# Feed-forward of two stacked transformer blocks: low halves of the summed x blocks moved from GpSimd to VectorE, and one block product of the first pair of units in whole fp32

## What is computed

```python
def first_block(x, ...):
    for l in range(DEPTH):                      # DEPTH = 2
        x = x + FFN_HALF * swiglu(rmsnorm(x, ffn1_norm[l]), ffn1_w_in[l], ffn1_w_out[l])
        x = x + hybrid_mixer(rmsnorm(x, mix_norm[l]), ...)
        x = x + FFN_HALF * swiglu(rmsnorm(x, ffn2_norm[l]), ffn2_w_in[l], ffn2_w_out[l])
    return x

def swiglu(h, w_in, w_out):
    gate, up = jnp.split(h @ w_in, 2, axis=-1)  # 1024 -> 2 x 2816
    return (jax.nn.silu(gate) * up) @ w_out     # 2816 -> 1024
```

## Time and profile before

| | before |
|---|---|
| median of 3 runs | 2645.51 us (2645.24 to 2645.69) |
| profiled execution | 2645.64 us, its span 2643.5 us |
| PE busy | 2615.1 us (99%), 16043 matmuls |
| PEld busy | 2307.5 us (87%) |
| DVE busy | 2036.6 us (77%) |
| ACT busy | 1551.3 us (59%) |
| POOL busy | 212.3 us (8%) |
| HBM read | 466.09 MB |

### The profile page before, as it was taken

One profiled execution on the slowest core, in us unless ns is written; L12 is line 12 of the kernel. 1 busy time (PEld: TensorE's weight loads), 2 busy tenths in 40 slices (PEclk: granted clock), 3 DMA queues, 4 the chain that ended last, 5 costly groups with the idle time before them and its releaser, 6 DMA issues.

```text
span 2643.5 us, 38649 instructions
## 1 busy us (share of the span) xinstructions
PE 2615.1 (99%) x16043; PEld 2307.5 (87%) x16043; DVE 2036.6 (77%) x2041; ACT 1551.3 (59%) x1707; POOL 212.3 (8%) x178
## 2 busy tenths in 40 slices
PE   9999999999999999999999999999999999999998
PEld 7889999978878899999788789999788789999787
DVE  8887754698799687447998995676997995676887
ACT  6656674465555567644556555555655555655654
POOL 1000170010010003400101000000100100000100
PEclk9999999999999999999999999999999999999999
DMA  6746555466465555545656465544755646543673
GB/s 214 240 156 199 162 149 170 136 215 229 153 226 175 168 167 156 177 133 182 227 168 230 158 206 179 152 144 152 238 192 189 201 160 192 161 135 129 218 234 105
DMA packets 394925, 474.23 MB, mean 179 GB/s; under 512 B 28855, under 2 KB 360959, under 8 KB 394496
## 3 DMA queue, kind: packets, MB, share of 16 engines
q1 hardware_dynamic: 390334, 469.86, 54.9%
q10 hardware_dynamic: 4418, 1.90, 0.3%
HBM read 466.09 MB, written 5.64 MB: 178 GB/s over the span
## 4 chain that ended last, share of the span: by engine, by line
PE 86%; DVE 9%; ACT 2%; issue 1%; DVEq 1%; DMA 0%; ACTq 0%; SPq 0%
PE bank L421 26%; PE bank L423 26%; PE bank L422 26%; DVE w_lo L1207 2%; PE bank L983 1%; DVE w_lo L408 1%; DVE conv_acc L2142 1%; PE bank L563 1%; ACT w_hi L1103 1%; DVE sum_t_t L1257 1%; PE bank L1806 1%; PE bank L1782 1%; DVEq L2944 0%; DVE part L2942 0%; DVEq L2146 0%
## 5 line engine op out<-in xcount | busy, mean ns | idle before, releaser
L421 PE MATMUL bank<-w_hi,xn_hi 128*128 128x512 f32 (+2 forms) x1664 | 599.5, 360 | 0.4
L423 PE MATMUL bank<-w_hi,xn_lo 128*128 128x512 f32 (+2 forms) x1664 | 589.9, 355 | 0.0
L422 PE MATMUL bank<-w_lo,xn_hi 128*128 128x512 f32 (+2 forms) x1664 | 589.3, 354 | 0.0
L408 DVE TENSOR_TENSOR w_lo<-raw,w_hi 128x2048 fp32r<-128x2048 f32 (+2 forms) x190 | 411.9, 2169 | 199.6 <-ACT w_hi L402 199.2
L1207 DVE TENSOR_TENSOR w_lo<-raw,w_hi 128x2048 fp32r<-128x2048 f32 x192 | 448.5, 2336 | 8.7 <-ACT w_hi L1103 8.6
L1103 ACT ACTIVATE w_hi<-raw 128x2048 fp32r<-128x2048 f32 x192 | 367.2, 1912 | 135.4 <-DMA raw<-in_ffn_w_out 42.1
L402 ACT ACTIVATE w_hi<-raw 128x2048 fp32r<-128x2048 f32 (+3 forms) x199 | 359.6, 1807 | 71.9 <-PE bank L423 69.4
L421 PE MATMUL bank<-xn_hi,w_hi 128*128 128x256 f32 (+1 forms) x1376 | 396.9, 288 | 1.0 <-DVE w_lo L408 1.0
L422 PE MATMUL bank<-xn_lo,w_hi 128*128 128x256 f32 (+1 forms) x1376 | 389.0, 283 | 0.0
L423 PE MATMUL bank<-xn_hi,w_lo 128*128 128x256 f32 (+1 forms) x1376 | 389.0, 283 | 0.0
L421 PEld LDWEIGHTS bank<-w_hi,xn_hi 128*128 128x128 f32 x1664 | 315.0, 189 | 46.0 <-issue 2.9
(11 more groups left out here) (392 smaller groups left out, 4262.8 us busy)
## 6 DMA issues: line engine op xcount, KB each, us to landing
raw<-in_w_in SPq DMA_DIRECT2D x122, 1024.0 KB, 5.3
raw<-in_ffn_w_in SPq DMA_DIRECT2D x126, 512.0 KB, 5.3
raw<-in_ffn_w_out SPq DMA_DIRECT2D x44, 1024.0 KB, 5.1
raw<-in_ffn_w_down SPq DMA_DIRECT2D x44, 1024.0 KB, 5.1
raw<-in_ffn_w_gate SPq DMA_DIRECT2D x64, 512.0 KB, 4.5
raw<-in_ffn_w_up SPq DMA_DIRECT2D x64, 512.0 KB, 5.6
block<-in_ffn_w_in SPq DMA_DIRECT2D x48, 512.0 KB, 7.2
block<-in_ffn_w_gate SPq DMA_DIRECT2D x24, 512.0 KB, 6.6
```

The costliest lines, as they stand in the source:

```text
L408: dve.tensor_tensor(in_order(kind, slot, w_lo), as_loaded(kind, slot), in_order(kind, slot, w_hi).bitcast(F32), ALU.subtract).then_inc(s_l ...
L421: pe.matmul(out, a_hi, b_hi, start=start, stop=False, skip_group_check=check)
L422: pe.matmul(out, a_hi, b_lo, start=False, stop=False, skip_group_check=check)
L423: return pe.matmul(out, a_lo, b_hi, start=False, stop=stop, skip_group_check=check)
```

## The change

The low halves of the four summed x blocks are made on DVE. `mixed_lo(0)` and `mixed_lo(1)` stand in the first ones, `mixed_lo(3)` and `mixed_lo(2)` in the first pair. ACT makes the four high halves in one go, in the order 0, 1, 3, 2, ahead of the first hidden unit's high half. `t3` of the first pair is no item any more: it is neither split nor given a slot. PE multiplies the sum `mixed[2]` with the sum of weights in `b12`, both in float32, in four matmuls (`whole_product`) that count a semaphore of their own, `s_whole`, on which the reload of `b12` and the sum `u3` wait. The list of items has 41 entries. ACT takes `hi` of dn 1 between its two gates of unit 1. GpSimd's program keeps only the first mixer's work.

```diff
+WHOLE = ("t3", TWOS[0])
@@ ffn_items
-            out += [("b11", u)] + downs + [(k, u) for k in ("b21", "t1", "t2", "b22", "t3", "t4")]
+            out += [("b11", u)] + downs + [(k, u) for k in ("b21", "t1", "t2", "b22", "t3", "t4") if (k, u) != WHOLE]
@@ raw_freed
-            i = self.items.index(("t3" if u == TWOS[0] else "b22", u))
+            i = self.items.index(("t4" if u == TWOS[0] else "b22", u))
@@ ffn_sp, other_blocks
-                block(b12, 0, u + 1, p.base + (FFN_AT["t3", u - 3] + 1 + START), s_block12)
+                if ("t3", u - 3) == WHOLE:
+                    block(b12, 0, u + 1, f + 1, s_block12, s_whole)
+                else:
+                    block(b12, 0, u + 1, p.base + (FFN_AT["t3", u - 3] + 1 + START), s_block12)
@@ ffn_pe
+            def whole_product(u, b):
+                pe.wait_ge(s_sums, count(SUMS, f, u, "t3"))
+                pe.wait_ge(s_xsum, mixed_count(f, 2))
+                weights = slot_view(b12, 4, 512)
+                for k in range(4):
+                    mm = pe.matmul(bank[b][:, :], mixed[2][:, k, :], weights[:, k, :], start=False, stop=k == 3,
+                                   skip_group_check=True)
+                mm.then_inc(s_whole, 1)
@@ two (PE)
                 pe.wait_ge(s_outs, count(OUTS, f, u, "u2"))
-                block_product("t3", u, 4, *x_mixed(2), False)
+                if ("t3", u) == WHOLE:
+                    whole_product(u, 4)
+                else:
+                    block_product("t3", u, 4, *x_mixed(2), False)
@@ first_ones (ACT)
                 hi("dn", 0)
-                mixed_hi(0)
+                for i in HALVED:
+                    mixed_hi(i)
                 hi_hidden(0)
-                mixed_hi(2)
                 hi("b11", 2)
-                gates(1)
+                first_gate(1)
                 hi("dn", 1)
-                mixed_hi(1)
+                second_gate(1)
                 hi_hidden(1)
-                mixed_hi(3)
@@ two (ACT and DVE)
-                hi("t3", u)
+                if ("t3", u) != WHOLE:
+                    hi("t3", u)
@@ first_ones (DVE)
                 lo("dn", 0)
+                mixed_lo(0)
                 lo_hidden(0)
                 sum_t1(2)
                 lo("b11", 2)
                 hide_from_bank(1, 0)
+                mixed_lo(1)
                 hide_from_bank(1, 1)
@@ two (DVE)
                     hide(u, 0, bank[4][:, 256:512], gate_act[:, 0, :])
+                    mixed_lo(3)
                     lo("b22", u)
                     sum_t4(u)
@@
-                lo("t3", u)
+                if ("t3", u) != WHOLE:
+                    lo("t3", u)
@@
                 dve.tensor_tensor(u2[:, :], bank[5][:, :], u2[:, :], ALU.add).then_inc(s_outs, 1)
+                if ("t3", u) == WHOLE:
+                    mixed_lo(2)
                 lo("g0", u + 2)
-                used("t3", u)
+                if ("t3", u) == WHOLE:
+                    dve.wait_ge(s_whole, f + 1)
+                    dve.wait_ge(s_xsumlo, halved_count(f, 2))
+                else:
+                    used("t3", u)
@@
-        def ffn_pool(pool, p, f):
-            def mixed_lo(i):
-                pool.wait_ge(s_xsumhi, mixed_count(f, i))
-                pool.tensor_tensor(mix_lo[i][:, :, :], mixed[i][:, :, :], mix_hi[i][:, :, :].bitcast(F32),
-                                   ALU.subtract).then_inc(s_xsumlo, 1)
```

More of the change, by code:

```diff
@@ L328, in build @@
         s_xsum = sem("x_blocks_mixed")
+        s_whole = sem("whole_sum_used")
         s_xsumhi = sem("x_mixed_hi")
@@ L901, in build @@
         MIXED = (0, 2, 1, 3)
-        MIXED_LO = (0, 1, 3, 2)
+        HALVED = (0, 1, 3, 2)
         def count(kinds, f, u, kind):
@@ L909, in mixed_count, with halved_count @@
             return 4 * f + MIXED.index(i) + 1
-        def mixed_lo_count(f, i):
-            return 4 * f + MIXED_LO.index(i) + 1
+        def halved_count(f, i):
+            return len(HALVED) * f + HALVED.index(i) + 1
         def ffn_pe(pe, p, q, f):
@@ L973, in x_mixed @@
             def x_mixed(i):
-                pe.wait_ge(s_xsumlo, mixed_lo_count(f, i))
+                pe.wait_ge(s_xsumlo, halved_count(f, i))
                 return (lambda k: mix_hi[i][:, k, :]), (lambda k: mix_lo[i][:, k, :])
@@ L1106, in gate, with first_gate, second_gate, gates @@
                 act.activation(dst, src, ACT.Silu, scale=rstd[:, t:t + 1]).then_inc(s_gact, 1)
-            def gates(u):
+            def first_gate(u):
                 act.wait_ge(s_gu, f * len(ONES) + ONES.index(u) + 1)
                 gate(u, 0, bank[gate_bank(u)][:, 0:256], gate_act[:, 0, :])
+            def second_gate(u):
                 act.wait_ge(s_used, p.base + (FFN_AT["g1", u] + 1 + START))
                 gate(u, 1, bank[gate_bank(u) + 1][:, 0:256], gate_act[:, 1, :])
+            def gates(u):
+                first_gate(u)
+                second_gate(u)
             def hi_hidden(u):
@@ L1263, in mix, with mixed_lo @@
                 dve.tensor_tensor(mixed[i][:, :, :], in0, in1, op).then_inc(s_xsum, 1)
+            def mixed_lo(i):
+                dve.wait_ge(s_xsumhi, halved_count(f, i))
+                dve.tensor_tensor(mix_lo[i][:, :, :], mixed[i][:, :, :], mix_hi[i][:, :, :].bitcast(F32),
+                                  ALU.subtract).then_inc(s_xsumlo, 1)
             def first_ones():
@@ L1354, in ffn_dve @@
             return update, lo_hidden_rows
-        def ffn_pool(pool, p, f):
-            def mixed_lo(i):
-                pool.wait_ge(s_xsumhi, mixed_count(f, i))
-                pool.tensor_tensor(mix_lo[i][:, :, :], mixed[i][:, :, :], mix_hi[i][:, :, :].bitcast(F32),
-                                   ALU.subtract).then_inc(s_xsumlo, 1)
-            for i in MIXED_LO:
-                mixed_lo(i)
         def out_pe(pe, p, j0, ready, count, sizes):
@@ L2336, in mixer1_pool @@
         def mixer1_pool(pool, l):
-            pool.wait_ge(s_rest, 16 * n_rest)
             for p in range(4):
@@ L3120, in _ @@
         def _(pool):
-            for b, l in layers:
-                for k in range(2):
-                    ffn_pool(pool, in_layer(plans[b], 3 * k, l), ffn_index(b, l, k))
-                    if k == 0 and b == 0:
-                        mixer1_pool(pool, l)
+            pool.wait_ge(s_rest, 16 * n_rest)
+            for l in range(LAYERS):
+                mixer1_pool(pool, l)
 def kernel(**inputs):
```

## The result

The kernel after the change takes 2719.87 us (median, 2718.62 to 2721.91), the kernel before 2645.38 us beside it: a ratio of 1.0284, 95% interval 1.0271 to 1.0296. That is 74.5 us more, slower by 2.8%. The profiled execution is one of 2718.62 us with a span of 2716.8 us, 73.0 us above the profiled one of before; the two spans differ by 73.3 us. The time lies inside the range of 2691 to 2723 and 10 us above the forecast of 2709.5.

The account below looks back on a forecast made before the run. The prediction took PE's work plus its waits to bound the kernel. From 2645.64 us it summed -1.6 (first pair) + 41.8 + 14.7 (borders) + 9 (clock) = +63.9 us to 2709.5 us, range 2691 to 2723.

Parts of the forecast that it names:

- The slots: Seven phase borders: items 0 and 1 newly wait for dn 9 and dn 10; loss 41.8 us into mixers, 14.7 into feed-forwards.
- Rival C: Phase borders: only the first of each border's two new waits costs; 34 us loss, 2678 us; chance 0.06.
- Rival D: Not slower: borders hide their waits and PE's 1.6 us before t3 return whole; 13 us gain, 2633 us; chance 0.04.
- The first pair: Each feed-forward's first pair: the wait before t3 goes, u3 becomes the wait; gain 0.2 us each, 1.6 us in all.
- a bound for `mixed_lo(2)`: First pair: if DVE's mixed_lo(2) found a hole, the gain would be 0.9 us each, 7 us in all.
- Rival E: First pair: whole float32 matmuls expose their overhang and more, t3 taking 5.3 us; 14 us over A, 2723 us; chance 0.05.
- The reloads: Reloads of b21's raw slot and b12, issued about 2 us later: nothing; up to 2 us per feed-forward if cover were gone.
- The clock: Borders into a mixer: PE's gaps lower TensorE's clock, 3 us at each of three of four borders, 9 us loss.
- The idle time of about 1.5 us: Borders into a mixer: PE's expected second idle spell, after one of 5 to 6 us and before one of 3 us.
- A: Main case: the border chain holds and the clock falls at most mixer borders; 2709.5 us; chance 0.50.
- B: Borders: the chain is right but the clock holds; 2645.6 + 54.9 = 2700.5 us; chance 0.33.
- The low halves on DVE: Low halves of the x sums: mixed_lo(0) and mixed_lo(1), 0.7 us each, fall in DVE's waits; costed at nothing.

Follow-up runs that it names:

- e1: The changed kernel with slots behind t2 counted as if t3 kept its place, so dn 8, 9, 10 end as before the change; 2657.01 us.
- e2: e1 with dn 8 and dn 9 swapping slots, so only item 0 of the next phase gets a later wait (for dn 9); 2691.10 us.
- e3: e1 with dn 9 in slot 3 and dn 10 in slot 1, so only the next phase's item 1 waits later (for dn 10); 2686.28 us.
- e8: e6 with mixed_lo(2) moved from behind c12 to ahead of the low half of t4; 2640.16 us, ratio to before 0.9982.
- e6: e1 with dn 2's load into b21's raw slot waiting for the sum for t4, not for t4's low half; 2643.18 us.
- e9: The changed kernel with dummy matmuls of zeros, 44 and 26, filling PE's two gaps at each border into a mixer; 2720.74 us.
- e4: The changed kernel with t3 still split and in its slot, keeping only the low halves on DVE and ACT's new order; 2644.20 us.
- e11: e3 with dummy matmuls of zeros, 26 ahead of a mixer's first matmul and 22 ahead of a following feed-forward's; 2682.10 us.

## Why the prediction was right in its mechanism and 10 us short

**The slots.** Right. e1 takes off 62.9 us by the numbering alone, where the borders with their clock were to cost 65.5. The chain of durations worked out from rows of before holds to 0.2 us at each of its four points in the border shown. Clock taken out, the sums are 41.5 for 41.8 and 15.1 for 14.7. Rival C is refuted by e2 and e3, where each wait costs alone and the two add. Rival D (the borders hide their waits) falls with the same runs.

**The first pair.** The mechanism is right: `t3` without a wait, its price 3.43 us for 3.44, `u3` as the new wait, 0.5 us where 0.7 was said, and a gain of 0.2 us for each feed-forward, as predicted. One premise was misread: the low half of b22 at 579.91 has no idle time ahead of it in the earlier trace rows, so it hadn't waited for another engine. In the kernel after it does, 0.72 us for ACT behind `mixed_lo(3)`, and starts at 592.05 - 12.26 = 579.79 by before's time, so the sum wasn't touched. The hole that I gave as a bound for `mixed_lo(2)` exists (1.38 us, in the first pair's rows). With it filled the pair gains the 0.9 us of the bound in e8, to 0.1 us, and by e8 against e6 that is worth 3.0 us of time. Rival E is refuted by the rows of `t3`.

**The reloads, costed at nothing. This step failed.** I wrote that their readers come 4 us or more later. I had taken the time from a load's issue to its reader for cover. The row of before says otherwise: ACT had stood 4.64 us in front of the high half of dn 3, released by its DMA. There was no cover on ACT. What cover there was lay behind it, in PE's queue, and was used up. I had also looked at the readers of the two reloads and not at the reader of what is queued behind them, though I named the item. The landmarks give 12.7 us, 1.6 us for each feed-forward and 3.8 at the most. e1 over before is 12.1 us with the first pair's gain taken off, and e1 over e6, where the reload alone differs, 13.8. My sign that each feed-forward between the borders would be as long as before within 0.5 us failed with it. My own bound, "up to 2 us" for each if the cover were gone, would have given up to 16. It should have been a term of the sum. With the measured 12.7 us in it the forecast would have been 2722.2. That the time still fell inside the range is luck: I had widened the range for errors in the steps of the borders, these came out within 1 us together, and the room was taken by a term that I hadn't counted.

**The clock.** The size was near (9 predicted, 6.4 measured), and that is luck too. That the clock falls at the mixer borders was right, at four of four behind the first gap (slow matmuls from 197.32, 923.54, 1646.73 and 2272.91), where I took three. What it costs there was mis-sized: I charged 3 us for a border, for step 2, step 3 and the transposes, and all four together cost 3.2, since step 2's slow products lie mostly in a wait for DVE and step 3 ran at full pace at three of them. The idle time of about 1.5 us that I had named as a sign between the two gaps isn't there in the kernel after, because the slow products fill it; with the clock kept up it is (1.18 us in e9). The other 3.2 us came at the borders into a feed-forward, which I had left out because their gaps are short. The Trainium skill's page "TensorE: Matmul & The Clock Gate", section "HAM oscillation — how this bites in real kernels", has, in its example, each wait inside PE's work bring the clock down. The rows agree behind the gaps of 4.8 and 5.5 us, four of four; behind the shorter ones it is two of four (3.0 and 3.4 us) and two of three (1.7 and 2.9 us), so there the rule is right in direction and not each time. Between A and B the case is A by its slow matmuls, but not by A's price.

**The low halves on DVE.** Costed at nothing, and e4 has nothing (0.9997, 0.9988 to 1.0006).

What stays open: why the late dn 3 costs some 2.2 us in some feed-forwards (the fourth here) and about 1 us in others. The 3.8 us of the third are the same and a fall of the clock: in e1, where this stretch has no slow matmul, it costs 2.2 us, and the eight matmuls at half pace in the kernel after make up the other 1.6. Nor do the runs say why some borders bring the clock down and others, with the same gap, don't.

## What to carry to other kernels

Where buffers are numbered by an item's place in a list, taking one item out re-aims every wait behind it, across the end of the phase too; compare the last numbers of a phase with the first of the next, since there nothing may be left to hide a wait. Before a moved load is costed at nothing, look up what released the reader, and the reader of the next load in the queue: if it stood waiting for a DMA already, there is no cover to spend. And a slow clock costs only where the slow work itself is what the rest waits for: count it from one fixed point to the next with the clock low and kept up, not by the number of slow matmuls.

## What the runs showed of the hardware

**The lower clock came behind gaps of 1.7 and 2.9 us, sometimes.** Into feed-forward 2, PE's timeline of the kernel after:

```profile
730.29 0.66 PE L566 MATMUL bank<-consts,x_gained 128*128 128x128 f32 x4 [1.70 <-DVE x_gained L541]
...
735.69 0.47 PE L424 MATMUL bank<-w_hi,xn_hi 128*128 128x512 f32 x1 [2.92 <-DVE xn_lo L546]
...
736.23 0.62 PE L426 MATMUL bank<-w_hi,xn_lo 128*128 128x512 f32 x1
736.64 0.63 PE L424 MATMUL bank<-w_hi,xn_hi 128*128 128x512 f32 x1
```

Behind two gaps of 1.70 and 2.92 us the first matmuls still follow at 0.23 us, and then eight, from 736.23 on, at 0.43 us, with a granted clock of 0.50 (737 to 739 us, half speed, the level of 1.2 GHz). Behind the third border of this kind, with the same gaps, there is none. Even one gap of 1.90 us ahead of the way down was followed by eight slow matmuls, from 808.04 on. Behind the gaps of 5.5 and 4.8 us at the mixer borders matmuls at half pace followed each time, four of four in the kernel after and four of four in e2.

**Zeros keep the clock up.** 26 dummy matmuls of 128 columns in a gap and 22 in the others left no slow matmul behind in e11.

**GpSimd and VectorE slow each other.** In the kernel before, the three low halves on GpSimd take 9.48 us, 3.2 each, where the same pass at 732.71 takes 1.29 and one of this shape from other tiles 1.04 (L2343), and a DVE pass of 128x2048 beside them 3.38 us in place of 2.28. GpSimd and then DVE:

```profile
563.56 9.48 POOL L1362 TENSOR_TENSOR x_mixed_lo<-x_mixed,x_mixed_hi 128x512 fp32r<-128x512 f32 x3 [7.10 <-ACT x_mixed_hi L1130]
```

```profile
571.82 3.38 DVE L1207 TENSOR_TENSOR w_lo<-sum_t_t,w_hi 128x2048 fp32r<-128x2048 f32 x1
```

Whether both go slower throughout or take turns isn't shown: if each were held for the other's whole pass, the sum would be 2.28 + 1.04 = 3.3 us for either, about what both take (my estimate from these rows). On DVE the same low half takes 0.68 us. All four cost 2.7 us of DVE there. Three DVE passes beside GpSimd in feed-forward 1 were 0.5, 1.1 and 1.1 us longer than 2.28, 2.7 us too, which may be why e4 comes out at no change; that wasn't tried apart.

**A whole float32 matmul** of 128x128 by 512 columns takes 0.86 us of PE in a row of four, where the three products of a split one take 0.68.
